# Order of the attention steps in a hybrid decoder layer, and when its deferred normalization is issued

## The reference

```python
def diff_attention(q, k, v, lam):        # q, k: (B,S,8,2,64), v: (B,S,8,128)
    s = einsum('bqhcd,bkhcd->bhcqk', q, k) * 64 ** -0.5
    s = where(qpos >= kpos, s, min)       # causal
    p = softmax(s, axis=-1)
    a = p[:, :, 0] - lam * p[:, :, 1]
    return einsum('bhqk,bkhe->bqhe', a, v)
o = rms_norm(o, subln_w, 1e-5) * (1 - lam_init)
o = o.reshape(B, S, 1024) * silu(z_a)
```

## Time and profile before

| what | value |
|---|---|
| time, three runs | 1262.53 us median (1262.22 to 1278.6) |
| the profiled execution | 1258.71 us, of which the slowest core's span is 1256.9 us |
| spans of the eight cores | 1250.4 to 1256.9 us |
| granted clock, mean, by core | 0.984 to 0.986 |
| attention stage on the slowest core | about 491 to 803 us |
| PE busy in that stage | 290.5 of 312 us |
| DVE and ACT busy in that stage | 180.0 and 178.5 us |

### The profile page before, as it was taken

The page is one execution under the profiler, slowest core; times in us unless marked ns, Lnnn a source line. Parts: engine busy times, 40 slices in busy tenths (PEclk is TensorE's granted clock), DMA queues, the critical chain, the costliest instruction groups (busy, mean ns, idle before and its releaser), DMA issues.

```text
span 1256.9 us, 21435 instructions; the slowest of 8 cores (1250.4 to 1256.9 us)
## 1 busy us (share of the span) xinstructions
PE 1169.6 (93%) x7900; PEld 646.7 (51%) x7900; DVE 577.9 (46%) x1270; ACT 377.5 (30%) x495; POOL 102.1 (8%) x196
## 2 busy tenths in 40 slices
PE   1878998899999999998999998999999999999996
PEld 1444554686444458765767544544444444444442
DVE  5654677414843322357554676633333333331443
ACT  3523444322011013555555555411111111111211
POOL 0110101010100110000000000110111011000000
PEclk9989999899999999999999999999999999999998
DMA  7858798245373363022020224353664586406633
GB/s 192 228 107 192 171 209 167 65 70 107 83 136 72 74 126 91 27 42 52 27 60 27 60 35 68 44 93 67 101 98 75 97 134 107 89 7 167 201 145 123
DMA packets 51365, 126.85 MB, mean 101 GB/s; under 512 B 5824, under 2 KB 12096, under 8 KB 48064
## 3 DMA queue, kind: packets, MB, share of 16 engines
q0 software_dynamic: 27648, 62.93, 31.8%
q1 hardware_dynamic: 23328, 62.44, 16.0%
q10 hardware_dynamic: 288, 0.11, 0.0%
HBM read 171.33 MB, written 17.04 MB: 150 GB/s over the span
## 4 chain that ended last, share of the span: by engine, by line
PE 82%; DVE 7%; DMA 4%; issue 3%; ACT 3%; SPq 0%; DVEq 0%; ACTq 0%
PE ps L1116 18%; PE ps L680 13%; PE ps L648 13%; PE ps L1165 9%; PE ps L516 5%; PE ps L797 5%; PE ps L1126 4%; PE ps L1120 4%; PE ps L768 3%; PE ps L885 3%; PE ps L562 2%; DMA r<-usc 2%; DVE zoz L841 1%; PE ps L477 1%; DMA r<-xo 1%
## 5 line engine op out<-in xcount | busy, mean ns | idle before, releaser
L1116 PE MATMUL ps<-hTo,wring 128*128 128x512 bf16 x1024 | 226.2, 379 | 0.0
L172 POOL DMA_DIRECT2D wring<-wp x176 | 93.4, 544 | 945.4 <-PE ps L768 305.8
L1116 PEld LDWEIGHTS ps<-hTo,wring 128*128 128x128 bf16 x1024 | 100.2, 98 | 120.6
L778 ACT ACTIVATE r<-ps 128x1024 bf16<-128x1024 f32 (+1 forms) x128 | 122.7, 967 | 89.8 <-PE ps L768 84.8
L516 PE MATMUL ps<-hTo,wring 128*128 128x384 bf16 x768 | 135.6, 339 | 13.6 <-ACT hTo L431 5.2
L1133 ACT ACTIVATE zoz<-zoz 128x512 f32<-128x512 f32 x64 | 40.2, 629 | 279.2 <-DVE zoz L1131 279.2
L648 PE MATMUL ps<-wring,hTo 128*128 128x256 bf16 x1024 | 120.4, 273 | 1.2 <-PE ps L768 1.2
L797 PE MATMUL ps<-r 128*128 128x129 bf16 x1216 | 101.5, 221 | 17.4 <-DVE small L821 7.8
L516 PEld LDWEIGHTS ps<-hTo,wring 128*128 128x128 bf16 x768 | 76.7, 101 | 71.3 <-issue 26.8
L680 PE MATMUL ps<-hTo,wring 128*128 128x512 bf16 x512 | 111.8, 379 | 0.0
L648 PEld LDWEIGHTS ps<-wring,hTo 128*128 128x128 bf16 x1024 | 96.5, 98 | 20.5 <-issue 9.7
(11 more groups left out here) (129 smaller groups left out, 1134.1 us busy)
## 6 DMA issues: line engine op xcount, KB each, us to landing
wring<-wp POOLq DMA_DIRECT2D x176, 256.0 KB, 7.1
r<-usc SPq DMA_DIRECT2D x32, 287.2 KB, 5.8
zoz<-xt SPq DMA_DIRECT2D x16, 512.0 KB, 6.5
hTx<-wop POOLq DMA_DIRECT2D x8, 1024.0 KB, 15.9
hTo<-xr SPq DMA_DIRECT2D x8, 1024.0 KB, 7.2
out<-hTo SPq DMA_DIRECT2D x16, 512.0 KB, 3.1
r<-xo SPq DMA_DIRECT2D x10, 768.0 KB, 8.7
ks<-r SPq DMA_DIRECT2D x32, 128.0 KB, 2.3
```

The costliest lines, as they stand in the source:

```text
L172: eng.dma_start(out=it[1][0], in_=it[1][1]).then_inc(self.dsem[it[2]], 16)
L778: t.op('act', lambda e: e.activation(out=et[:, :, 0:w], in_=src, func=AF.Exp, scale=0.125), reads=[('ps', pb), ('ps', pb + 1)], writes=[(' ...
L1116: t.op('pe', lambda e, dc=dc, k=k, w=w, o=o, cs=cs, tg=tg: e.matmul(o[k], lhsT=w[:, dc, cs], rhs=rhs512(dc, tg), start=(dc == 0), stop=(dc ...
```

## The change

A slot's list of steps begins with the all-or-nothing block, then the diagonal, then the full blocks. In slot 0 the diagonal is thereby the last of two steps. The flag that ends an accumulation is set for that case too. `run_late` is no longer called in the first and in the last step of a slot, and in the others it takes up to five operations in place of four. Nothing is added to or taken from the work.

```diff
-                lst = [('own', s)] + [(k, x) for x in range(s) for k in ('own', 'oth')] + [('oth', s)]
+                lst = [('oth', s), ('own', s)] + [(k, x) for x in range(s) for k in ('own', 'oth')]
                 for n, (kind, x) in enumerate(lst):
                     pairs.append((h, s, kind, x, n == 0, n == len(lst) - 1))
...
             for k, sub in todo:
                 o = 256 if diag and k == 1 else 256 * k + 128 * sub
                 for c in range(2):
-                    end = last and k == 1 and c == 1
+                    end = last and c == 1 and (k == 1 or (1, sub) not in todo)
...
             for n in range(len(pairs)):
                 if n + 2 < len(pairs):
                     emit_qk(n + 2)
-                run_late(4)
+                if not (pairs[n][5] or pairs[n][4]):
+                    run_late(5)
                 yield 1.0
                 emit_pv(n)
```

## The result

The changed kernel takes 1296.28 us (median of 4 runs, 1294.39 to 1297.27), against 1262.38 for the kernel before, measured again beside it. The ratio is 1.0268, 95% interval 1.0254 to 1.0281. Slower by 33.9 us; predicted were 30.4 more and 1293. In some executions cores of a die run at a lower granted clock for a part of the program or all of it, and the time is longer (up to 1468.66 us for the kernel before, at 0.81); medians are of all executions, ratios and intervals leave the clearly longer ones out.

A forecast was written before the change was run, and what follows sets the result against it. PE, busy in 93% of the span, was taken as the bound, through its work or waits. Waits +23.5, clock +8.2 and other edits -1.3 gave +30.4 us, on 1262.5 a forecast of 1293 us, range 1278 to 1304.

The forecast's parts named there:

- The count: Before slot 1's copy of banks 4 and 5: 19 deferred operations forced in place of 5, in 7 of 8 heads.
- The length of the burst: End of slot 1: the 19 forced operations take 5.04 us on DVE after the mask, before the copy.
- t: The start of the last step of slot 1, from which the mask, the copy and PE's resume are timed.
- The seven waits: First value matmul behind slot 1, heads 1 to 7: PE waits 32.1 us for DVE, against 8.6 before, +23.5.
- The upper bound of +26: Highest addition to the seven waits, should the short operations run at the slower spacing of 0.345 us.
- The other edits: Copies at other ends of slots, freed by leaving out run_late, and masks nearer the copy: net -1.3 us.
- the stage's start: The attention stage's first slot: its start needs no mask, -0.3 us.
- First in, first out: DVE's queue is strictly in order, so the copy can't pass the 19; the whole of +23.5 stands.
- The clock: After each of the seven waits PE runs at 1.2 GHz: 1.4 us each, 9.8, less 1.6 already paid, +8.2.
- a rival, at 0.1: Lower clock level lasts twice as long behind the seven waits: 3.2 us each, +43 in all, 1306; chance 0.1.

The follow-up runs named there:

- late_alone: Kernel before with its old step order, but run_late skipped in first and last steps and up to five operations in the others: 1297.00 us, ratio 1.0262.
- late_nine: Changed kernel with run_late(9) in place of run_late(5), so 11 operations, not 19, are forced before the copy: 1301.93 us, ratio 1.0254.
- busy_wait_2: Changed kernel with idle matmuls filling PE's seven long waits, only the last of each set signalling: 1288.96 us, ratio 1.0177.
- order_alone: Changed kernel with run_late(4) called in every step as before, leaving the new order of the steps alone: 1270.07 us, ratio 1.0081.
- old_best: Kernel before with run_late(5) except in a slot's last step, and only operations reading the copy's buffer forced before it: 1255.95 us, ratio 0.9955.
- copy_first: Changed kernel, forcing before the copy only those deferred operations that read the buffer it overwrites: 1267.72 us, ratio 1.0051.

## Why the prediction was right

Point by point:

- *The count.* 19 operations forced before the copy of slot 1, in seven heads: the timeline shows them, and late_alone shows that the edit to `run_late` alone brings the loss.
- *The length of the burst.* Predicted: mask at t + 1.4, PE at t + 7.9. Measured t + 1.41 and t + 7.7. With the gate's chain, predicted were masks at t + 3.4 in head 2 and t + 3.6 in head 7, measured t + 3.5 and t + 3.7. The 19 took 548.37 - 543.47 = 4.9 us, predicted 5.04.
- *The seven waits.* Predicted 4.4, 5.4, 4.4, 3.4, 4.4, 4.5, 5.6 for heads 1 to 7, sum 32.1. Measured 4.36, 5.39, 4.36, 3.18, 4.37, 4.71, 5.69, sum 32.06. The three with the gate's chain were right too, which late_nine confirms by what it leaves nearly unchanged. The upper bound of +26 is too low by its own reasoning: 0.07 us more for each of nine operations in seven heads is +28.
- *The other edits.* Predicted -1.3, 0.3 of it at the stage's start and 1.0 at the other waits. Measured is about -0.9, and its parts are further off than the sum. The waits went from 3.66 to 2.36, -1.3. The one of 1.64 us in head 7 did not go but stayed at 0.38, the one of 0.54 went, and the ends of heads rose by 0.5 in place of 1.2 (0.73, 0.51 and 0.74, before 0.74, none and 0.74). The stage's start, from its first score matmul to its first value matmul, did not get shorter but went from 2.5 to 3.0 us: no mask stands there, but the third set of scores waits 1.20 us for the longer exponential of the first step, before 0.84. That these misses nearly cancel is luck.
- *First in, first out.* The forecast rested on the copy not passing the 19, by the row and by the Trainium skill (TensorE: Matmul & The Clock Gate, the section on the array's architecture). The trace agrees: in head 1 the copy starts only as the last L841 ends, 3.5 us after PE had begun to wait.
- *The clock.* Here the size was off. The term was "1.4 each: 9.8". busy_wait_2 measured 14.5 us for the seven, 2.1 each. The price per fall was right for a single one: 1.6 us in the kernel before, where the stage is 309.4 us on four cores with a fall after the 2.27 us wait and 307.8 on three without, 1.4 to 1.6 in order_alone, 1.3 in old_best. But the lower level lasted twice as long behind most of the waits (the window from 592.5 to 597 us is at 0.51 from end to end): a single fall is (1 - 0.58) x 4 us x 2 = 3.4 us at the lower level, seven of them would be 24, and the stage has 42. I had given the longer one to a rival, at 0.1; it had the length right for most of them and the price too high (3.2 each), since the 42 us are as much as twelve single falls and cost 14.5 us, 1.2 for each of the twelve. Net of the fall paid before, it is about 12.6 us in place of 8.2. The Trainium skill, TensorE: Matmul & The Clock Gate, section on HAM oscillation, tells of a kernel in which every long wait was followed by the lower clock. The trace agrees with one exception: core 3 has a fall at each of its seven long waits, but core 5 has none behind the 3.23 us of head 4 (granted clock 1.00 from 679 to 687 us).

So 22.3 of the 34.9 us are waits of L797, predicted 22.2 with the start, and 12.6 are nearly all the clock, predicted 8.2. That 4.4 us is the distance between 30.4 and what the stage shows; the medians differ by 33.9.

Not settled: why a fall follows one wait of 2 us and not another of the same length. Before the change four cores had one after a wait of 2.27 us and one core after 1.63 us, and three went through both waits without any. In order_alone, core 0 had none after two of its waits of 1.84 us nor after 2.32 us. The length of the last wait alone doesn't decide it, and no run here shows what does.

## What to carry to other kernels

Work that is put off into an engine's free time must have a way to be done before the point that forces it. Count the queue's intake and its outlets for each stage, the forced remainder above all: 5 or 19 operations before one copy made the difference of 34 us, while DVE was busy for 180 of the stage's 312 us. Give a forced flush the narrowest condition that safety needs, and let nothing deferred stand between the last input and the operation that the busiest engine waits for. And price a new wait of TensorE with the slow stretch behind it: here 32 us of waits cost 14.5 us more by the clock, and such stretches can be longer than the one that a single row shows.

## What I had not expected of the hardware

- Waits of 1.84 us (order_alone) and 1.95 us (copy_first) were followed by a stretch at 1.2 GHz, though before the change three cores went through 2.26 us without one, and after it one core through 3.23 us.
- Filling the waits with idle matmuls kept the clock at full and made the stage 14.5 us shorter, with the same work done and the same copies late.
- Matmuls of 512 columns into one bank took 0.52 us each when each waited for the signal of the one before, and 0.216 when only the last of the set signalled.
